# A hybrid attention layer on Trainium2: the MLP's two products by Strassen's seven block products, and scores of two heads in turn

## The reference, cut to what matters

```python
h = rms_norm(x) * (1.0 + scale1) + shift1
proj = h @ w_in[l]
...
s = jnp.einsum('bnqhgd,bnkhd->bhgnqk', qb, k2) * (dh ** -0.5) + bias
...
o = jnp.einsum('bhgnqk,bnkhd->bnqhgd', p, v2)
...
x = x + gate1 * mix
h = rms_norm(x) * (1.0 + scale2) + shift2
x = x + gate2 * (jnp.square(jax.nn.relu(h @ w_mlp_in[l])) @ w_mlp_out[l])
return rms_norm(x) * final_norm_g
```

## Time and profile before

| | |
|---|---|
| median of 3 runs (lowest, highest) | 1196.06 us (1194.1, 1196.11) |
| the profiled execution | 1196.62 us, its span 1194.8 us |
| TensorE busy | 1136.0 us, 95% |
| VectorE busy | 563.2 us, 47% |
| ScalarE busy | 377.1 us, 32% |
| GpSimd busy | 65.3 us, 5% |
| moved by DMA | 87.49 MB |

### The profile page before, as it was taken

One profiled execution on the slowest core, in us unless ns is written; L12 is line 12 of the kernel. 1 busy time (PEld: TensorE's weight loads), 2 busy tenths in 40 slices (PEclk: granted clock), 3 DMA queues, 4 the chain that ended last, 5 costly groups with the idle time before them and its releaser, 6 DMA issues.

```text
span 1194.8 us, 13898 instructions
## 1 busy us (share of the span) xinstructions
PE 1136.0 (95%) x5347; PEld 914.4 (77%) x5347; DVE 563.2 (47%) x859; ACT 377.1 (32%) x717; POOL 65.3 (5%) x72
## 2 busy tenths in 40 slices
PE   1799999999999999999999999999999999999995
PEld 1678866766677887788888888888888888888884
DVE  6667555687776426422432422422423423424436
ACT  1630101467666115543214113114123124033023
POOL 0002110021322000000000000000000000000001
PEclk9999999999999998899999999999999999999998
DMA  9838540100003511111121121111211211211103
GB/s 357 253 116 289 194 142 1 36 1 1 1 1 108 175 36 36 36 49 58 36 71 36 36 70 35 60 46 35 70 35 35 70 35 35 70 36 36 53 1 140
DMA packets 56629, 87.49 MB, mean 73 GB/s; under 512 B 13987, under 2 KB 34956, under 8 KB 56588
## 3 DMA queue, kind: packets, MB, share of 16 engines
q1 hardware_dynamic: 51820, 70.09, 17.9%
q0 software_dynamic: 4768, 16.82, 4.0%
HBM read 82.69 MB, written 4.21 MB: 73 GB/s over the span
## 4 chain that ended last, share of the span: by engine, by line
PE 90%; DVE 4%; ACT 2%; DMA 1%; SPq 1%; issue 1%; DVEq 0%; ACTq 0%
PE bank L487 39%; PE bank L512 29%; PE bank L617 14%; PE bank L683 2%; DMA x_in<-in_x 1%; PE bank L659 1%; PE bank L648 1%; PE bank L582 1%; DVE act_lo L930 1%; PE bank L736 1%; SPq L297 1%; DVE act_full L928 0%; PE bank L610 0%; DVE x_nrm L917 0%; DVE x L1286 0%
## 5 line engine op out<-in xcount | busy, mean ns | idle before, releaser
L487 PE MATMUL bank<-act_hi,w_hi 128*128 128x512 f32 x672 | 264.0, 393 | 0.4 <-issue 0.4
L487 PE MATMUL bank<-act_lo,w_hi 128*128 128x512 f32 x672 | 262.7, 391 | 0.0
L487 PE MATMUL bank<-act_hi,w_lo 128*128 128x512 f32 x672 | 262.6, 391 | 0.0
L1321 ACT ACTIVATE w_hi<-raw 128x2048 fp32r<-128x2048 f32 x45 | 86.2, 1916 | 446.8 <-PE bank L512 209.4
L512 PE MATMUL bank<-w_hi,hid_hi 128*128 128x512 f32 x512 | 199.2, 389 | 0.0
L512 PE MATMUL bank<-w_lo,hid_hi 128*128 128x512 f32 x512 | 199.2, 389 | 0.0
L512 PE MATMUL bank<-w_hi,hid_lo 128*128 128x512 f32 x512 | 199.2, 389 | 0.0
L1203 DVE TENSOR_TENSOR hid_lo<-bank,hid_hi 128x512 fp32r<-128x512 f32 x64 | 44.2, 691 | 238.9 <-ACT hid_hi L1519 238.9
L1231 DVE TENSOR_TENSOR x<-bank,x 128x512 f32<-128x512 f32 x120 | 81.2, 689 | 153.9 <-PE bank L512 153.5
L487 PEld LDWEIGHTS bank<-act_hi,w_hi 128*128 128x128 f32 x672 | 127.2, 189 | 27.3 <-issue 0.9
L487 PEld LDWEIGHTS bank<-act_lo,w_hi 128*128 128x128 f32 x672 | 127.0, 189 | 26.5 <-issue 0.2
(11 more groups left out here) (167 smaller groups left out, 1031.2 us busy)
## 6 DMA issues: line engine op xcount, KB each, us to landing
ada_w<-in_w_ada POOLq DMA_DIRECT2D x32, 512.0 KB, 6.8
raw<-in_w_mlp_in SPq DMA_DIRECT2D x64, 256.0 KB, 3.3
raw<-in_w_mlp_out SPq DMA_DIRECT2D x64, 256.0 KB, 3.3
raw<-in_w_in SPq DMA_DIRECT2D x36, 256.0 KB, 4.8
ada_w_first<-in_w_ada SPq DMA_DIRECT2D x8, 1024.0 KB, 10.8
x_in<-in_x SPq DMA_DIRECT2D x8, 512.0 KB, 15.5
raw<-in_w_out SPq DMA_DIRECT2D x16, 256.0 KB, 4.7
x<-in_x SPq DMA_DIRECT2D x8, 512.0 KB, 4.3
```

What stands on the lines that cost most here:

```text
L487: mm = pe.matmul(bank[2 * half + m][:, :], w, act(b)[:, k, half * HALF:half * HALF + HALF], start=(n == 0), stop=(n == 3 * KT - 1))
L1321: a.activation(w_hi[:, par, :], raw[:, par, :], ACT.Copy).then_inc(s_hi, 1)
```

## The change

**Scores.** `front(n, r)` now goes through heads 2r and 2r + 1 of both groups, a head of the lower and a head of the upper 64 partitions in turn, and the two groups write to two banks. Bias, sinks and the operand of `attend` are rearranged to match.

**The MLP.** Each product is made of 2 x 2 blocks and by seven products of blocks in place of eight (Strassen's scheme in Winograd's form), with sums of blocks before and after. GROUP, the pairs and the loop are gone; all of up comes before all of down.

- *Up*: h is cut by width and by token half into 11, 12, 21, 22. VectorE makes four sums T1 to T4 of them, in float32, once; all seven forms stay in SBUF as high and low parts. The weights come in 8 units u of two times 256 columns; VectorE makes four sums of each unit's four blocks, and each unit has seven products (P1, P2, P5, P6, P7, P4, P3), each of two halves m of 12 matmuls. Products that are added up accumulate in one PSUM bank pair (X, Y, Z); between them ScalarE copies the running value out (`kept`), and VectorE adds from the other pair (`up_add`). Relu and square follow, then VectorE makes four sums of the hidden blocks (`hidden_sums`). SyncE stores all seven hidden forms in memory (`hid`, 3.7 MB a unit).
- *Down*: 28 steps n, four (q) for each of seven products. A step has 48 matmuls (4 k x 4 token tiles x 3). SyncE loads the hidden form (1 MB) for it; ScalarE makes high parts of it and of the weight block (`down_hi`), VectorE the low parts (`down_lo`), in two buffers: the high part of n waits for the end of step n - 2. Weight blocks 11, 12 and 22 stay in SBUF and are summed in place (`down_sums`, in iterations 4 to 7); those of P2, P4 and P3 come through a ring of two.
- *x1* is stored in memory after the output projection and loaded again at n = 15, since its place is used. gate2 is now applied to results (`gated_add`, `last_add`), not to weights. The final norm of tokens 512 to 1023 stands in iteration 25, that of the rest after the last step.

```diff
+NP = 7
+X_UP, Y_UP, Z_UP = (4, 2), (3, 6), (0, 1)
+UP_BANKS = (X_UP, Y_UP, Z_UP, X_UP, X_UP, X_UP, Z_UP)
+UP_STARTS = (True, True, True, False, False, False, False)
+UP_H = ("11", "21", "T1", "T2", "T3", "T4", "22")
+H_ORDER = ("11", "21", "T1", "T2", "T3", "22", "T4")
+UP_P1, UP_P2, UP_P5, UP_P6, UP_P7, UP_P4, UP_P3 = range(NP)
+HID_11, HID_12, HID_S1, HID_S2, HID_S3, HID_22, HID_S4 = range(NP)
+
+
+NQ = 4
+NS = NP * NQ
+X_DOWN, Y_DOWN = (3, 6, 5, 7), (0, 1, 2, 4)
+DOWN_HID = (HID_11, HID_12, HID_S2, HID_S1, HID_S3, HID_22, HID_S4)
+DOWN_BANKS = (X_DOWN, Y_DOWN, X_DOWN, Y_DOWN, X_DOWN, X_DOWN, Y_DOWN)
+DOWN_STARTS = (True, True, False, True, False, False, False)
+DN_P1, DN_P2, DN_P6, DN_P5, DN_P7, DN_P4, DN_P3 = range(NP)
+
+
+PAIR_OF = (0, 2, 1, 3)
...
+                sp.wait_ge(s_free, G_O + 8 + t + 1)
+                sp.dma_start(x1_rows[:, t, :], x1[:, t, :]).then_inc(s_x1_out[t // 4], 16)
+            sp.wait_ge(s_hlo, 2 * NP)
+            up_load(1)
+
+            def hid_sums_store(u):
+                for i, form in enumerate((HID_S1, HID_S3, HID_S2, HID_S4)):
+                    sp.wait_ge(s_hid_sum, 4 * u + i + 1)
+                    hid_store(form, u)
+
+            def hid_store_ready(form, u):
+                sp.wait_ge(s_hid[form], u + 1)
+                hid_store(form, u)
...
+            def dn_h_load(n):
+
+                p, q = n // NQ, n % NQ
+                sp.wait_ge(s_hid_out[DOWN_HID[p]], 16 * (2 * q + 2))
+                if n >= 2:
+                    sp.wait_ge(s_dlo, 2 * (n - 2) + 1)
+                for j in range(2):
+                    sp.dma_start(hid_raw[n % 2][:, 2 * j:2 * j + 2, :],
+                                 hid[DOWN_HID[p], 4 * q + 2 * j:4 * q + 2 * j + 2].rearrange("m p c -> p m c"))\
+                        .then_inc(s_dn_h[n % 2], 16)
+
+            def dn_load(dst, block_of, q, landed):
...
+            def dn_ring_load(r):
+
+                q = r % NQ
+                if r >= 2:
+                    step = (NQ * DN_P2, NQ * DN_P4, NQ * DN_P3)[(r - 2) // NQ] + (r - 2) % NQ
+                    sp.wait_ge(s_dlo, 2 * step + 2)
+                dn_load(dn_ring[r % 2], ((1, 0), (1, 0), (1, 1))[r // NQ], q, s_dn_ring[r % 2])
+
+            for u in range(NU):
+                if u > 0:
+                    hid_sums_store(u - 1)
+                hid_store_ready(HID_11, u)
+                if u + 2 < NU:
+                    sp.wait_ge(s_wlo, NP * (u + 1))
+                    up_load(u + 2)
+                if u == NU - 1:
+                    dn_h_load(0)
+                    sp.wait_ge(s_prod, 14 * u + 2 * UP_P5 + 2)
+                    for q in range(2):
+                        dn_load(dn_c[:, q], (0, 0), q, s_dn_c[q])
+                    dn_h_load(1)
+                hid_store_ready(HID_22, u)
+                if u == NU - 1:
+                    sp.wait_ge(s_prod, 14 * u + 2 * UP_P7 + 2)
+                    for q in range(2, NQ):
+                        dn_load(dn_c[:, q], (0, 0), q, s_dn_c[q])
...
+            for n in range(4, NS):
+                dn_h_load(n)
+                if n in (4, 6):
+                    dn_ab_load(n // 2)
+                if 6 <= n < 8:
+                    dn_ring_load(n - 4)
+                if n == NQ * DN_P5 + 3:
+                    sp.wait_ge(s_dlo, 2 * (NQ * DN_P5 + 4))
+                    for t in range(NT):
+                        sp.dma_start(x1[:, t, :], x1_rows[:, t, :]).then_inc(s_x1[t // 4], 16)
+                    sp.dma_start(gain[:, :], final_norm_g.rearrange("(a d) -> a d", a=1).broadcast_to([P, D]))\
+                        .then_inc(s_gfin, 16)
+                if NQ * DN_P4 - 2 <= n < NS - 2:
+                    dn_ring_load(4 + n - (NQ * DN_P4 - 2))
+            for t in (4, 5, 6, 7, 0, 1, 2, 3):
+                sp.wait_ge(s_fin, (t - 4) % NT + 1)
                 sp.dma_start(out_d[:, t, :], x1[:, t, :]).then_inc(s_out, 16)
...
+            def front(n, r, first=False):
+
+                if not first or r > 0:
+                    pe.wait_ge(s_sc_free, 4 * n + 2 * r)
+                for j in range(2):
+                    for g in range(HEADS // 4):
+                        q = q_t[g * DH:(g + 1) * DH, 2 * r + j, tok(n)]
...
+            def up_product(u, i, m):
+
+                f = NP * u + i
+                name = UP_H[i]
+                b = bank[UP_BANKS[i][m]][:, :]
...
+                        pe.wait_ge(s_c12, 2 * (u - 1) + m + 1)
+                elif i == UP_P6:
+                    pe.wait_ge(s_p1, 2 * u + m + 1)
+                elif i == UP_P7:
+                    pe.wait_ge(s_u2, 2 * u + m + 1)
+                elif i == UP_P4:
+                    pe.wait_ge(s_u3, 2 * u + m + 1)
+                else:
+                    pe.wait_ge(s_c22, 2 * u + m + 1)
+                n = 0
+                for k in range(4):
+                    if u == 0 and m == 0 and k % 2 == 0:
+                        pe.wait_ge(s_hlo, 2 * H_ORDER.index(name) + k // 2 + 1)
+                    for x, y in ((0, 0), (0, 1), (1, 0)):
+                        mm = pe.matmul(b, (up_hi, up_lo)[x][f % 4][:, k, m * P:(m + 1) * P],
...
+            for n in range(NS - 1):
+                p, q = n // NQ, n % NQ
+                pe.wait_ge(s_dlo, 2 * n + 2)
+                for k in range(4):
+                    for t in range(4):
+                        if q == 0 and k == 0:
+                            bank_ready(p, t)
+                        mm = down_matmuls(n, k, t, DOWN_STARTS[p] and q == 0 and k == 0, q == NQ - 1 and k == 3)
+                if q < NQ - 1:
+                    mm.then_inc(s_step, 1)
+            pe.wait_ge(s_dlo, 2 * NS)
+            for t in range(4):
...
+            def hidden_sums(u):
+
+                h11, h12, h21 = (hid_sb[n][:, :, :] for n in (HID_11, HID_12, HID_S3))
+                h22, s1, s2, s4 = (hid_sb[n][:, :, :] for n in (HID_22, HID_S1, HID_S2, HID_S4))
+                for n in (HID_11, HID_S3, HID_22, HID_12):
+                    v.wait_ge(s_hid[n], u + 1)
+                v.wait_ge(s_hid_out[HID_S1], 16 * u)
+                v.tensor_tensor(s1, h21, h22, ALU.add).then_inc(s_hid_sum, 1)
+                v.tensor_tensor(h21, h11, h21, ALU.subtract).then_inc(s_hid_sum, 1)
+                v.wait_ge(s_hid_out[HID_S2], 16 * u)
+                v.wait_ge(s_hid_sum, 4 * u + 1)
+                v.tensor_tensor(s2, s1, h11, ALU.subtract).then_inc(s_hid_sum, 1)
+                v.wait_ge(s_hid_out[HID_S4], 16 * u)
+                v.wait_ge(s_hid_sum, 4 * u + 3)
...
+            def wide_hi(f):
+
+                u, i = f // NP, f % NP
+                if i in (0, 1, 5):
+                    a.wait_ge(s_raw[u % 2], RAW_DONE[u % 2] + LAND * (u // 2 + 1))
+                else:
+                    a.wait_ge(s_wsum, 4 * u + (1, 3, 2, None, 4)[i - 2])
+                if f >= 4:
+                    a.wait_ge(s_prod, 2 * (f - 3))
+                elif f >= 2:
+                    a.wait_ge(s_full, G_END)
+                a.activation(up_hi[f % 4][:, :, :], up_form(f), ACT.Copy).then_inc(s_whi, 1)
+
+            def next_hi(f):
+                if f < NP * NU:
...
+            for u in range(NU):
+                f = NP * u
+                if u > 0:
+                    wide_hi(f + 3)
+                    relu_squared(HID_S3, u - 1, s_c12)
+                    wide_hi(f + 4)
+                if u == 0:
+                    a.wait_ge(s_x1_out[0], 64)
+                for m in range(2):
+                    kept(HID_11, u, m, UP_P1, s_p1)
+                if u == 0:
+                    for k in range(0, KT, 2):
+                        affine(1, k)
+                    form_hi("T1")
+                    form_hi("T2")
+                    wide_hi(4)
+                    form_hi("T3")
+                wide_hi(f + 5)
+                relu_squared(HID_11, u, s_c11)
+                if u == 0:
+                    form_hi("22")
+                wide_hi(f + 6)
+                kept(HID_S3, u, 0, UP_P6, s_u2)
+                kept(HID_S3, u, 1, UP_P6, s_u2)
+                if u == 0:
+                    form_hi("T4")
+                next_hi(f + 7)
+                if u == NU - 1:
+                    down_hi(0)
+                kept(HID_22, u, 0, UP_P7, s_u3)
+                kept(HID_22, u, 1, UP_P7, s_u3)
+                next_hi(f + 8)
+                relu_squared(HID_22, u, s_c22)
...
+                if n + 1 < NS:
+                    down_hi(n + 1)
+                if n == 25:
+                    for i in range(4):
+                        final_square(i, 4 + i)
+                    for i in range(4):
+                        final_root(i)
```

More of the change, by code:

```diff
@@ new lines, in _, with down_matmuls @@
+            for u in range(NU):
+                for i in range(NP):
+                    for m in range(2):
+                        up_product(u, i, m)
+                        if u == 0 and (i, m) in ((UP_P1, 1), (UP_P2, 0)):
+                            turn(1, range(4 * i, 4 * i + 4))
```

(67 more changed lines are left out.)

683 lines of the change are left out of this document (437 added, 246 removed).

## The result

| | before | after |
|---|---|---|
| median of 4 runs (lowest, highest) | 1196.09 us (1194.1, 1197.54) | 1163.25 us (1162.09, 1166.35) |
| the profiled execution, its span | 1196.62, 1194.8 us | 1166.35, 1164.5 us |

After takes 0.9718 of the time of before, 95% interval 0.970 to 0.9736: 32.8 us less, where the sum of the forecast was 38.9 (1158, range 1128 to 1186). The profiled execution of after is its longest of four; span against span the gain is 30.3 us.

What follows compares the result with a forecast made beforehand. The prediction took TensorE to bound the kernel (busy 95% of the span), so each matmul less was worth 0.2267 us. Its terms summed to -38.9, from 1196.6 to 1157.7, said as 1158 us, range 1128 to 1186.

Steps and rivals of the forecast that it cites:

- 384 matmuls fewer: MLP up and down: 2688 matmuls in place of 3072, at 0.2267 us each, -87.1 us.
- scores: Attention turns: score calls of two heads in turn fall from 1.92 to 1.1 us, -8.5 us in all.
- head of the MLP, clock: Unit 0: VectorE's forms and unit 1's weights hold P4 until 526.3, +13.6 us; slow clock after it, +2.
- up units, VectorE in steps 4 to 7: Up units steady without waits, 0; VectorE's 11.45 us a step against 10.88 in down steps 4 to 7, +0.4.
- up to down: Down steps 2 and 3 wait for hidden tiles queued behind other transfers after the last up product, +4.9 us.
- x1 at step 16, clock: Down step 16: its hidden tile is issued behind x1 and gain, +7.8 us; slow clock, +2.
- steps 22 to 27, clock: Late down: ring order makes steps 14.7 us, +18.5; step 27 behind VectorE's finishing of four tiles, +4.3; slow clock, +2.
- tail: After the last matmul: VectorE's added gate2 product and add per tile, last scale ends after 11.0 us, +1.2.
- rival C: Up units: slow landing of stored hidden forms makes each of 7 units some 6 us longer, 1199 us; chance 0.10.
- Rival B: MLP: loads land later under mixed traffic and VectorE's head and tail chains are 20% longer, 1185 us; chance 0.13.
- Rival A: MLP: feeding is hidden, the ring costs nothing and x1 and the restart little, 1108 us; chance 0.10.
- Rival D: Down steps 22 to 27 run wholly at half clock, 20.5 us each, 1193 us; chance 0.05.

Runs made afterwards that it cites:

- split_pool_late: After with four issue-order edits, unit 2's weights loaded later, unit 1's in halves, and GpSimd's first work of a turn held until VectorE has normalised: 1107.22 us.
- u2_first: After with unit 0's two copies of U2 out of PSUM put first in ScalarE's order: 1164.97 us, ratio 0.9725 to before.
- ring_order: After with the hidden tile of step n + 1 issued ahead of the wait and load of the ring block: 1138.72 us, ratio 0.9516 to before.
- split_u2_first: After with four issue-order edits, unit 2's weights later, unit 1's in halves, and unit 0's U2 copies first on ScalarE: 1110.78 us, ratio 0.9277 to before.

## Why the prediction was right

The forecast was faster by 38.9 us; the profiled executions differ by 30.3 in span, the medians by 32.8. By the steps of the prediction:

| step | predicted | in the trace of after | by its experiment |
|---|---|---|---|
| 384 matmuls fewer | -87.1 | -87.05 | |
| scores | -8.5 | -5.1 | -4.3 |
| head of the MLP, clock | +15.6 | +15.0 | +7.6 of it by order |
| up units, VectorE in steps 4 to 7 | +0.4 | 0 | |
| up to down | +4.9 | +7.3 | +7.2 |
| x1 at step 16, clock | +9.8 | +12.4 | +12.1 |
| steps 22 to 27, clock | +24.8 | +23.4 | +24.5 |
| tail | +1.2 | -0.7 | |

The trace's column is worked out from starts of steps less 10.88 us each, and for the scores from the first score call of the second block of tokens to the end of the last call (112.09 us before, 107.03 after). Without the scores the column makes -29.6. The output projection's last matmul starts only 0.58 us earlier (464.56 for 465.14), which makes -30.2: of the scores' gain 4.5 us were given back ahead of the MLP. The first score call came 1.7 later than in before (237.62 for 235.88), which lies within the spread of the opening; 16 transposes of 1.7 us together now stand ahead of that last matmul and not in the head; the last turn's wait for gla_out is 0.7; some 0.4 I have not taken apart.

**Fewer matmuls: right.** 1344 up and 1344 down at 0.2267 us, units 1 to 7 at 38.08 each without a wait. So rival C (round trip of the hidden forms) fell, and with it the one way to slower: a store of hidden forms lands in 3.2 us (median of 56), where 10 would have cost nothing.

**Scores: the overlap right, the size wrong.** I took 1.1 for a call and measured 1.07. But the prediction names as a sign of being wrong that 17.62 does not fall to about 16.5, and it fell to 17.09, so this term failed by its own test. The step that failed is that VectorE's work in a turn keeps its length and turns "about 0.5" of the second call into a wait. VectorE's busy time went from 13.21 to 13.59, since it now normalises while GpSimd works; split_pool_late parts the two and brings the turn to 16.67. That is 0.41 of the 0.57 missing at 16.52 (17.62 less 1.1). The rest is TensorE's wait, 0.7 us in the middle of the turn, at the transposes of gla_out, where I had 0.5 at its end. I had read VectorE's work without a gap off; a TensorE that comes sooner can wait anywhere in such a stretch, not only at its end.

**Head: the sum right, its inside partly wrong.** P1 began at 468.96, 2.2 us earlier than I worked out; P4 2.3 earlier. The one long wait before P4 was there, ended by ScalarE's copy behind the landing of unit 1's weights. But it was 10.7 us long, where the prediction's 510.5 to 526.3 makes 15.8: P4 began 2.3 earlier, and P7 ended 2.8 later (513.3). The prediction has no long wait before P7, and there was one of 6.0. ScalarE at that place in after:

```profile
502.38 1.99 ACT L1936 ACTIVATE h_hi<-h 128x1024 fp32r<-128x1024 f32 x2
504.27 1.04 ACT L1898 ACTIVATE up_hi<-up_raw 128x1024 fp32r<-128x1024 f32 x1
505.22 1.06 ACT L1961 ACTIVATE hid<-bank 128x512 f32<-128x512 f32 x2
...
522.34 1.06 ACT L1898 ACTIVATE up_hi<-up_raw 128x1024 fp32r<-128x1024 f32 x1 [12.28 <-DMA up_raw<-in_w_mlp_in]
523.30 1.07 ACT L1961 ACTIVATE hid<-bank 128x512 f32<-128x512 f32 x2
```

P7's first matmul stands at 505.90, just behind the copy of U2 at 505.22, which had form 22 and a weight form ahead of it in ScalarE's queue. That this wait was left out cost the sum nothing, as u2_first shows. The load itself took 10.8 us (issued 511.53, landed 522.3), not the 8.4 that I had from the rate of the earlier trace rows; but it was issued at 511.5 and not 516, so the two errors nearly met. That the sum came out is in part luck of this kind. P7 and P4 both began at the low clock, and took 7.41 and 8.38 us where 24 matmuls are 5.44. After the wait before P4 it was low for some 6 us, not the 4 of the earlier trace rows, and cost 2.9 where I had 2 (granted clock third from the end):

```profile
524.00:526.00 2.00, 2.00 (x5) 1.63 (x6) 2.00 (x3) 1.32 (x2) 0.00 (x0) 0.50 1.10 354
526.00:528.00 2.00, 2.00 (x7) 1.54 (x6) 2.00 (x3) 0.00 (x0) 0.00 (x0) 0.50 0.38 121
528.00:530.00 2.00, 2.00 (x6) 1.63 (x5) 2.00 (x3) 1.76 (x2) 0.00 (x0) 0.51 0.03 10
```

**Up to down, and x1: right in place and cause, each some 2.5 us too small.** At the start I had left out the clock (1.76 us). At x1 step 16 was late by 9.7 where I had 7.8: SyncE issued x1 and gain from 970.67 on, came to the hidden tile at 976.00, and it took 12.21 more to land, 18.2 us in all where I had 16.2. The low clock behind it cost 2.8, where I had 2.

**The ring: right, but two errors inside its row met.** Steps 22 to 26 came 14.3 to 15.5 us apart, I had 14.7; they make 19.9 us against 18.5. The landing was 7.55 and 6.78 us from the hidden tile's issue, the conversions 6.5. The prediction has 8.0 for the landing of both MB, but calls the first 5.4, which with 2.9 makes 8.3; from 685.84 to 691 it is 5.2. Measured from the first issue at 1052.57 to the landing at 1061.56 it is 9.0, and 8.2 in the next step. Step 27 made 3.3 and hardly any slow clock (0.2), where I had 4.3 and 2: VectorE's finishing of four tiles was the cause, as forecast, but took 9.7 us and not 10.6.
The Trainium skill ("DMA: Bandwidth & Descriptors", Anatomy of one DMA) would have 6.8 us for the 2.1 MB and a period of 13.5; its fit is for one DMA issued from GpSimd, and these are four issues of SyncE. The trace does not agree with it: the row of 1 MB, which I went by, was nearer.
Rival B (more waits of the same kind, 1185) held a little: landings in the head and at x1 came later than my rates said, by some 4 us in all, and the ring by 1.4, not 27. Rival A (the feeding is hidden) fell; ring_order shows why it could have held: with the same bytes, all six steps are hidden once the order is right. Rival D fell: the clock did go low at the start of steps 22, 24 and 26, which took 2.3, 2.8 and 1.8 us longer for it, but this only shortened the wait behind them (1.5, 1.2 and 1.5 us, against 4.5, 4.0 and 3.3 behind steps 21, 23 and 25); no step came 20.5 us after the one before.

**Tail: wrong in sign, small.** From the last matmul to the end it is 12.4 us against 13.1, where I had 1.2 more. All of it lies ahead of the last scale, which ends 9.3 us after the last matmul (before 10.1, forecast 11.0); from there to the end both kernels take 3.05. Why VectorE's walk is shorter than mine I have not taken apart.

## What to carry to other kernels

When a change removes matmuls from a kernel bound by TensorE, count them at their measured pitch, and then walk every issue order step by step: here 87 us were sure and some 60 of 92 came back, which TensorE's busy share (95% before, 91% after) hardly shows. Put a load in its queue by when it is needed and not by where its code stands: here each hidden tile behind 1 MB that was needed later cost 3.4 to 4.6 us, and moving three groups of issues, and a few instructions on ScalarE and VectorE, won 53 us. A wait is worth removing only if no other ends behind it: check by the engine that feeds both (u2_first, split_u2_first) before you count it. And before you give 1 or 2 us to an edit, see where the stage began in each trace.
